# Two weighted products instead of three in every projection of a one-core block kernel

## The chip, the cores and the metric

The kernel runs on one core of one Trainium2 chip. The metric is the device time of one execution in microseconds. A second number, the span, is the time from the first to the last instruction of the profiled execution.

## The reference, cut to what matters

One layer of a hybrid block on 512 tokens of width 1024, all in fp32. A combined projection of the normed input feeds three branches; each branch has a projection of its own and a gate; their sum goes through an output projection. Then a layer of 16384 single-neuron experts follows, of which each token picks 128.

```python
proj = xn @ w_in[l]
(sb_q, sb_k, sb_v, ml_q, ml_k, ml_v, ml_i, ml_f, ml_o, mem_q, gate_pre) = jnp.split(proj, splits, axis=-1)
...
qk = jax.nn.silu(_causal_conv(jnp.concatenate([ml_q, ml_k], axis=-1), conv_w[l], conv_b[l]))
...
merged = (gates[:, :, 0] * (y_sb @ w_sb_o[l]) + gates[:, :, 1] * (y_ml @ w_ml_o[l])
          + gates[:, :, 2] * (y_mem @ w_mem_o[l]))
h = h + merged @ w_out[l]
hn = _rmsnorm(h, g_ffn[l])
h = h + _peer(hn, w_peer_q[l], peer_k1[l], peer_k2[l], peer_u[l], peer_v[l])
```

## The kernel before, in words

TensorE multiplies in fp32r, which keeps fewer bits than fp32. So each operand is cut in two: a high part (the value rounded to fp32r) and a low part (what is left). A projection adds three products for each block: high by high, high by low, low by high (the list `PARTS`).

The weights come in 101 items of 128 x 1024 values (512 KB). Item n passes through these hands:

- SyncE issues its load into one of four buffers `w_raw` (`load_item`, L507), once the low part of item n-4 is made.
- ScalarE makes the high part (`high_w`, L1263) in one of two buffers `w_r`, once item n-2 is multiplied: that item had the same buffer.
- GpSimd makes the low part (`low_ws`, L453), once the high part is there; for seven of the items VectorE does it (`DVE_LOW`, L1593).
- TensorE multiplies it with 24 products of 128 x 128 by 128 x 512 (12 where it works for the 256 memory tokens, 16 for item 20), and its end counts up `item_done`.

The stages follow one another on TensorE in a fixed order written into the program:

- Items 0 to 3 (L722, L731): keys of the memory tokens. Between them the input x is turned by TensorE, its high part made by ScalarE (L1286), its low part by VectorE (L1620). The row of 1/rms of the tokens then makes a round trip through DRAM (L528, L530) to stand on all partitions, in `rstd_b`; no projection is taken out of PSUM before it is there. SyncE loads item 8 and what follows behind that round trip.
- Items 4 to 19 (`t_item`, L741, L790): transposed projections, one PSUM bank each, four banks in turn. VectorE takes each out (L1633, L1660). Item 20 (L823) holds the input and forget gate columns.
- Items 21 to 36 (`n_item`, L754): natural projections. Meanwhile VectorE does the causal convolution of eight 128 x 512 groups (`conv`, L1646 and L1649, four instructions each), and ScalarE the silu.
- Items 37 to 44: memory values (L754) and gate items (L741) in turn. Gate items 4 to 23 are spread among the attentions as filler for TensorE: three for each of four pairs of stick-breaking heads, five in the mLSTM, three in the attention on memory.
- A head pair of the stick-breaking attention runs: scores on TensorE (L883, L887); Abs, Exp, Ln on ScalarE (L1337 to L1343); VectorE's `keep` (L1736); high part on ScalarE (L1347) and low part on VectorE (L1751); suffix sums on TensorE (L899); Exp on ScalarE (L1352).
- Items 65 to 76 (`branch`, L1027): the three branch projections. VectorE multiplies with the gates (L1878), adds up (L1885) and makes the low part (L1890).
- Items 77 to 84 (L754, L1048): output projection, then the second norm (L1905, L1454, L1914).
- Items 85 to 100 (L702, L741): query projection; key scores (L1102); top 16 lists on VectorE (L1955 to L1965).
- 128 `up` tiles of 16 products (L1141), of which `N_TOP` = 56 run while VectorE finishes its lists; GpSimd makes their low parts (L495). Then one-hot products (L1179) among 48 more `up` tiles, the rest of the `up` tiles, and 128 `down` tiles (L1150). These two already use two products with weighted parts.

A waiting instruction holds up all that stands behind it on its engine.

Of the kernel before, what the change touches and what calls it, by code (L numbers as in the profile page):

```python
# [60 lines left out]
N_TOP, PER_BLOCK = 56, 12  # L61
# [12 lines left out]
PARTS = ((0, 0), (0, 1), (1, 0))  # L74
# [22 lines left out]
def weights_of(n):  # L97
# [3 lines left out]
    if n <= I_IF:  # L101
        return n - I_T
# [9 lines left out]
SILU_AFTER = {3: (0, 1), 6: (2,), 7: (3,), 10: (4,), 11: (5,), 14: (6,), 15: (7,)}  # L112
EXP_AFTER, TURN_AFTER = (10, 20, 31, 44), (20, 33, 45, 52)
# [12 lines left out]
def build(nc, A, out, gates_dram, pre_dram, acts_dram):  # L126
    ctx = ExitStack()
    with ctx:
# [85 lines left out]
        x_two = carve_r("x_two", 34816, 4096)  # L214
        h_scaled = carve("h_scaled", 22528, 4096)
        junk = carve("junk", 43008, 1024)
        u_raw = [carve(f"uraw{s}", at, 1024) for s, at in enumerate((12288, 13312, 22528, 23552))]
        u_pairs = [carve_r(f"u_r{s}", at, 2048) for s, at in enumerate((24576, 10240, 18432, 20480))]
        act_stage = carve("act_stage", 8192, 2048)
        qryT = carve("qryT", 26624, 2048)  # L220
        keysT = carve("keysT", 28672, 2048)
        scores = carve("scores", 30720, 1024)
# [86 lines left out]
        x2 = x_two.rearrange("p (k t) -> p k t", t=T)  # L309
# [35 lines left out]
        if_low, f_sum = sem("if_low"), sem("f_sum")  # L345
# [47 lines left out]
        x2_made = sem("x2_made")  # L393
# [27 lines left out]
        def _(pool):  # L421
# [77 lines left out]
        def _(sp):  # L499
# [31 lines left out]
            with sp.Fori(2, I_IF // 4) as i:  # L531
                for s in range(4):
                    load_item(i * 4 + s, s, -I_T)
# [1045 lines left out]
        def _(dve):  # L1579
# [31 lines left out]
            for k in range(2, KD):  # L1611
                mem_low(k)
# [585 lines left out]
```

## Time and profile before

| what | value |
|---|---|
| time, median of 3 runs | 1636.06 us (1635.29 to 1636.38) |
| time outside the span (median less span) | 1.56 us |
| profiled execution: span | 1634.5 us |
| TensorE busy | 1627.7 us (100%), 8198 products |
| VectorE busy | 1088.1 us (67%) |
| ScalarE busy | 751.5 us (46%) |
| GpSimd busy | 406.9 us (25%), none after the first half |
| mean DMA rate | 211 GB/s |

The profiled execution is not timed by itself; its span is set beside the median. Busy is the time in which an engine works on at least one instruction. Products are pipelined, so the time from one to the next is read from long rows of them, and not from the mean of one.

### The profile page before, as it was taken

The numbers are of one execution on the slowest core, as the hardware profiler recorded it, in microseconds if no ns is written. First come the engines' busy times: TensorE is split into PE (matmuls) and PEld (weight loads), VectorE is DVE, ScalarE is ACT, GpSimd is POOL, SyncE is SP. The second block draws the span as 40 slices with busy tenths as digits, with TensorE's granted clock in tenths as the row PEclk, the third lists the DMA queues.
The fourth block names the chain that finished last, engine by engine and source line by source line (L and its number), as shares of the span: only waits on it lengthen the run. The fifth ranks groups of instructions, "written<-read, shape, count | busy, mean of one in ns | idle before, by whom it ended". The sixth has DMA issues, their size and how long they took to land.

```text
span 1634.5 us, 23689 instructions
## 1 busy us (share of the span) xinstructions
PE 1627.7 (100%) x8198; PEld 1348.8 (83%) x8198; DVE 1088.1 (67%) x1890; ACT 751.5 (46%) x939; POOL 406.9 (25%) x185
## 2 busy tenths in 40 slices
PE   9999999999999999999999999999999999999999
PEld 7888878788788888888888888888888888888887
DVE  4128443357483678999989999934466666666665
ACT  5223246644543434455445555555444444444442
POOL 5435433243253435777740000000000000000000
PEclk9999999999999999999999999999999999999999
DMA  6222242222542231666658888898698888888884
GB/s 235 95 103 92 102 156 96 97 78 97 201 170 100 103 130 61 223 213 213 216 213 292 320 298 308 295 321 296 236 321 293 280 286 292 297 285 286 291 288 156
DMA packets 166420, 344.68 MB, mean 211 GB/s; under 512 B 13260, under 2 KB 78796, under 8 KB 164048
## 3 DMA queue, kind: packets, MB, share of 16 engines
q1 hardware_dynamic: 166352, 343.79, 60.6%
q8 instruction: 41, 0.67, 0.2%
q14 instruction: 27, 0.22, 0.0%
HBM read 268.24 MB, written 75.51 MB: 210 GB/s over the span
## 4 chain that ended last, share of the span: by engine, by line
PE 98%; POOL 1%; ACT 1%; DVE 0%; issue 0%; ACTq 0%; POOLq 0%
PE ps L1150 28%; PE ps L1141 27%; PE ps L741 18%; PE ps L754 8%; PE ps L1027 4%; PE ps L1179 4%; PE ps L899 1%; PE ps L689 1%; PE ps L1102 1%; POOL u_r L495 1%; PE ps L1048 1%; PE ps L883 1%; PE ps L909 1%; PE ps L945 1%; PE ps L935 1%; PE ps L722 0%
## 5 line engine op out<-in xcount | busy, mean ns | idle before, releaser
L1150 PE MATMUL ps<-v_r,w_pairs 128*128 128x512 f32 x2036 | 461.7, 389 | 0.0
L1150 PEld LDWEIGHTS ps<-v_r,w_pairs 128*128 128x128 f32 x2036 | 382.3, 188 | 79.2
L1141 PE MATMUL ps<-hT_r,u_r 128*128 128x512 f32 x1024 | 400.7, 391 | 0.1
L1141 PE MATMUL ps<-x_two,u_r 128*128 128x512 f32 x1024 | 398.7, 389 | 0.0
L453 POOL TENSOR_TENSOR w_r<-w_raw,w_r 128x1024 fp32r<-128x1024 f32 x92 | 234.2, 2547 | 372.4 <-ACT w_r L1263 370.1
L2104 DVE TENSOR_TENSOR v_r<-vraw,v_r 128x1024 fp32r<-128x1024 f32 x128 | 156.9, 1226 | 150.2 <-ACT v_r L1560 150.2
L1560 ACT ACTIVATE v_r<-vraw 128x1024 fp32r<-128x1024 f32 x128 | 135.7, 1060 | 254.0 <-PE ps L1150 248.6
L1141 PEld LDWEIGHTS ps<-hT_r,u_r 128*128 128x128 f32 x1024 | 192.3, 188 | 40.4 <-POOL u_r L495 0.5
L1141 PEld LDWEIGHTS ps<-x_two,u_r 128*128 128x128 f32 x1024 | 192.3, 188 | 39.4
L741 PE MATMUL ps<-xT_r,w_r 128*128 128x512 f32 x936 | 218.6, 392 | 0.0
L1263 ACT ACTIVATE w_r<-w_raw 128x1024 fp32r<-128x1024 f32 x99 | 104.3, 1057 | 245.5 <-PE ps L741 132.0
L741 PEld LDWEIGHTS ps<-xT_r,w_r 128*128 128x128 f32 x936 | 174.1, 188 | 37.1 <-issue 1.2
L1507 ACT ACTIVATE act_stage<-ps 128x512 f32<-128x512 f32 x128 | 76.6, 598 | 226.3 <-PE ps L1141 226.3
L495 POOL TENSOR_TENSOR u_r<-uraw,u_r 128x1024 fp32r<-128x1024 f32 x56 | 160.0, 2865 | 47.9 <-ACT u_r L1488 47.8
L1488 ACT ACTIVATE u_r<-uraw 128x1024 fp32r<-128x1024 f32 x128 | 134.9, 1054 | 13.4 <-DMA uraw<-in_u 13.4
L2066 DVE TENSOR_TENSOR u_r<-uraw,u_r 128x1024 fp32r<-128x1024 f32 x72 | 87.5, 1223 | 63.3 <-ACT u_r L1488 63.2
L2100 DVE TENSOR_TENSOR w_f<-act_in,g_in 128x512 f32<-128x512 f32 x128 | 87.5, 684 | 7.0 <-issue 5.9
L2107 DVE SCALAR_TENSOR_TENSOR w_pairs<-w_pairs,w_f 128x512 fp32r<-128x512 f32 x128 | 87.5, 684 | 0.0
L754 PE MATMUL ps<-w_r,xT_r 128*128 128x512 f32 x384 | 87.2, 389 | 0.0
L754 PEld LDWEIGHTS ps<-w_r,xT_r 128*128 128x128 f32 x384 | 72.1, 188 | 14.9
L741 PE MATMUL ps<-hT_r,w_r 128*128 128x512 f32 x360 | 83.9, 391 | 0.0
L1562 ACT ACTIVATE w_pairs<-w_f 128x512 fp32r<-128x512 f32 x128 | 78.7, 615 | 3.4 <-DVE w_f L2100 3.4
(266 smaller groups left out, 1700.4 us busy)
## 6 DMA issues: line engine op xcount, KB each, us to landing
uraw<-in_u SPq DMA_DIRECT2D x128, 512.0 KB, 4.8
vraw<-in_v SPq DMA_DIRECT2D x128, 512.0 KB, 5.4
w_raw<-in_w SPq DMA_DIRECT2D x100, 512.0 KB, 3.7
acts_out<-act_stage SPq DMA_DIRECT2D x128, 256.0 KB, 2.3
gates<-stage SPq DMA_DIRECT2D x16, 2048.0 KB, 7.4
g_in<-gates SPq DMA_DIRECT2D x64, 512.0 KB, 6.4
act_in<-acts_out SPq DMA_DIRECT2D x128, 256.0 KB, 5.3
gates_pre<-pre_stage SPq DMA_DIRECT2D x24, 256.0 KB, 2.3
```

The costliest lines, as they stand in the source:

```text
L453: pool.tensor_tensor(wr4[:, n % 2, 1, :], raw3[:, n % 4, :], wr4[:, n % 2, 0, :].bitcast(F32), ALU.subtract).then_inc(w_lo_ready, 1)
L495: pool.tensor_tensor(u2[n % 4][:, 1, :], u_raw[n % 4], u2[n % 4][:, 0, :].bitcast(F32), ALU.subtract).then_inc(u_lo, 1)
L741: ins = pe.matmul(bank(b), wr4[:, s, ww, k * P:(k + 1) * P], act[:, wa, k, :], start=k == 0 and ww + wa == 0, stop=k == KD - 1 and ww == 1)
L754: ins = pe.matmul(bank(b0 + t), act[:, wa, 2 * j + k, t * P:(t + 1) * P], wr4[:, s, ww, k * BANK:(k + 1) * BANK], start=j == 0 and k == 0 ...
L1141: ins = pe.matmul(bank(s % 2), u2[s][:, w, k * P:(k + 1) * P], x2[:, k, :] if w else hr4[:, 0, k, :], start=i == 0, stop=i == 15, skip_gro ...
L1150: ins = pe.matmul(bank(2 * q + h), w2[:, s, w, q * P:(q + 1) * P], v2[s][:, w, h * BANK:(h + 1) * BANK], start=start and w == 0, stop=stop ...
L1263: act.activation(wr4[:, q % 2, 0, :], raw3[:, q, :], ACT.Copy).then_inc(w_hi_ready, 1)
L1488: act.activation(u2[s][:, 0, :], u_raw[s], ACT.Copy, scale=KEEP).then_inc(u_hi, 1)
L1560: act.activation(v2[s][:, 0, :], vr[:, s, :], ACT.Copy, scale=KEEP).then_inc(v_hi, 1)
L2066: dve.tensor_tensor(u2[s][:, 1, :], u_raw[s], u2[s][:, 0, :].bitcast(F32), ALU.subtract).then_inc(u_lo_dve, 1)
L2100: dve.tensor_tensor(wf[:, s % 2, :].rearrange("p (b t) -> p b t", t=BLK), ai3[:, s, :].rearrange("p (b t) -> p b t", t=BLK), g4[:, par, :, ...
L2104: dve.tensor_tensor(v2[s][:, 1, :], vr[:, s, :], v2[s][:, 0, :].bitcast(F32), ALU.subtract).then_inc(v_lo, 1)
```

## The change

- Every projection adds two products: weights times 1 - 1/128 rounded (high) by the high part of the activation, and the rest of the weights (low) by a second activation part that is weighted with 128 so that the two products add up to the full one. `PARTS` goes. High and low product of a block stand side by side on TensorE.
- For x and the memory tokens VectorE now makes the second part in two instructions (`x_low`, `x_two`; `mem_low`, `mem_two`), both with their own counters. Elsewhere it is one instruction, with other constants; the separate `x_two` of the expert layer goes.
- A new counter `hi_used` rises with the last high product of an item, `item_done` with the last low one. `high_w` waits for `hi_used` of item n-2 and for that item's low part; `low_ws` and `low_w` wait for `item_done` of item n-2.
- The transposed items come in another order: q and k of the mLSTM first. The convolution moves from among the natural items to among the transposed ones (`CONV_AFTER`), silu with it.
- Item 20 is an ordinary `t_item`.
- Weights of the second norm are applied on VectorE with a row `g_row`, loaded by two more DMAs.
- `N_TOP` is 60 for 56, the key scores have 8 slots for 2, the lists are turned later (`TURN_AFTER`), and query items use banks in another order.

```diff
-N_TOP, PER_BLOCK = 56, 12
+N_TOP, PER_BLOCK = 60, 12
...
-PARTS = ((0, 0), (0, 1), (1, 0))
...
-SILU_AFTER = {3: (0, 1), 6: (2,), 7: (3,), 10: (4,), 11: (5,), 14: (6,), 15: (7,)}
-EXP_AFTER, TURN_AFTER = (10, 20, 31, 44), (20, 33, 45, 52)
+CONV_AFTER = {3: 0, 4: 1, 6: 2, 7: 3, 9: 4, 10: 5, 12: 6, 13: 7}
+EXP_AFTER, TURN_AFTER = (12, 24, 36, 49), (22, 35, 47, 56)
+SCORE_SLOTS = 8
...
                         pool.wait_ge(w_hi_ready, o * 4 + n)
+                        pool.wait_ge(item_done, o * 4 + (n - 1))
                         pool.tensor_tensor(wr4[:, n % 2, 1, :], raw3[:, n % 4, :], wr4[:, n % 2, 0, :].bitcast(F32),
...
             sp.dma_start(rstd_p, acts_dram[1, 0, :].partition_broadcast(P)).then_inc(row_in, 16)
...
+            sp.dma_start(acts_dram[2, 0:2, :].rearrange("a b -> (a b)").rearrange("(p k) -> p k", k=KD),
+                         cols[:, C_FFN:C_FFN + KD]).then_inc(row_out, 16)
+            for n in range(8, I_IF + 8):
                 load_item(n, n % 4)
...
+            def t_part(s, b, act, w, made=None):
+
+                for k in range(KD):
+                    if made is not None:
+                        pe.wait_ge(made, k + 1)
+                    ins = pe.matmul(bank(b), wr4[:, s, w, k * P:(k + 1) * P], act[:, w, k, :],
+                                    start=k + w == 0, stop=k == KD - 1 and w == 1)
+                ins.then_inc((hi_used, item_done)[w], 1)
+
             def t_item(n, s, b, act, made_by_dve=1):
 
+                high_ready(n)
                 take_item(n, made_by_dve)
                 for k in range(KD):
-                    for ww, wa in PARTS:
-                        ins = pe.matmul(bank(b), wr4[:, s, ww, k * P:(k + 1) * P], act[:, wa, k, :],
-                                        start=k == 0 and ww + wa == 0, stop=k == KD - 1 and ww == 1)
-                ins.then_inc(item_done, 1)
...
+                    for w in range(2):
+                        ins = pe.matmul(bank(b), wr4[:, s, w, k * P:(k + 1) * P], act[:, w, k, :],
+                                        start=k + w == 0, stop=k == KD - 1 and w == 1)
+                        if k == KD - 1:
+                            ins.then_inc((hi_used, item_done)[w], 1)
...
-                    pe.wait_ge(memT_out, KD)
+                    pe.wait_ge(low_made, KD)
...
-                at_least(act, item_done, n - 1)
-                act.activation(wr4[:, q % 2, 0, :], raw3[:, q, :], ACT.Copy).then_inc(w_hi_ready, 1)
+                at_least(act, hi_used, n - 1)
+                if n >= 2:
+                    wait_low_w(act, n - 2)
+                act.activation(wr4[:, q % 2, 0, :], raw3[:, q, :], ACT.Copy, scale=KEEP).then_inc(w_hi_ready, 1)
...
+                high_w(n, n % 4)
+                g = CONV_AFTER.get(n - I_T - 4)
+                if g is not None:
+                    act.wait_ge(conv_done, g + 1)
+                    act.activation(projT3[:, 8 + g, :], conv_out[:, g % 2, :], ACT.Silu).then_inc(silu_done, 1)
...
+            def x_two(k):
+                dve.wait_ge(low_made, KD + k + 1)
+                dve.scalar_tensor_tensor(out=xr4[:, 1, k, :], in0=xr4[:, 1, k, :].bitcast(F32), scalar=SPREAD,
+                                         in1=xr4[:, 0, k, :].bitcast(F32), op0=ALU.mult, op1=ALU.add).then_inc(xT_out, 1)
+
+            x_low(0)
+            for k in range(1, KD):
+                x_low(k)
+                x_two(k - 1)
+            x_two(KD - 1)
...
+            for j in range(NT):
+                g = (j + 8) % NT
+                dve.wait_ge(item_done, I_T + j + 1)
...
+                if j in CONV_AFTER:
+                    conv(CONV_AFTER[j])
...
-                    dve.tensor_scalar(hs3[:, t, half], h3[:, t, half], rstd[:, c_], None, ALU.mult).then_inc(h_normed, 1)
+                    dve.scalar_tensor_tensor(out=hs3[:, t, half].rearrange("q (k p) -> q k p", p=P),
```

## Rows read from the trace of the kernel before

**Rows 1.** The page: TensorE's granted clock in 40 slices, in tenths (9 is 90% or more).

```profile
PEclk9999999999999999999999999999999999999999
```

**Rows 2.** The chain that ended last, in order of time: start, length, what.

```profile
29.58 81.60 PE ps L741 x360
...
845.13 3.69 PE ps L1179 x64
...
1167.15 461.49 PE ps L1150 x2036
```

**Rows 3.** Timeline, 55 to 75 us: start, length, engine, line, what, idle before.

```profile
56.88 1.06 ACT L1263 ACTIVATE w_r<-w_raw 128x1024 fp32r<-128x1024 f32 x1 [4.44 <-PE ps L741]
...
58.02 2.40 POOL L453 TENSOR_TENSOR w_r<-w_raw,w_r 128x1024 fp32r<-128x1024 f32 x1 [3.10 <-ACT w_r L1263]
...
56.95 0.69 DVE L1660 TENSOR_TENSOR projT<-ps,rstd_b 128x512 f32 x1 [4.76 <-PE ps L741]
```

**Rows 4.** Timeline, 100 to 202 us: VectorE's convolution beside GpSimd.

```profile
137.99 4.34 DVE L1649 SCALAR_TENSOR_TENSOR work<-projT,cols,work 128x509 f32<-128x509 f32 x3
...
146.73 2.32 DVE L1649 SCALAR_TENSOR_TENSOR work<-projT,cols,work 128x509 f32<-128x509 f32 x3
148.97 2.63 DVE L1646 TENSOR_SCALAR work<-projT,cols 128x512 f32<-128x512 f32 x1
...
137.80 2.40 POOL L453 TENSOR_TENSOR w_r<-w_raw,w_r 128x1024 fp32r<-128x1024 f32 x1 [2.44 <-ACT w_r L1263]
...
148.68 2.63 POOL L453 TENSOR_TENSOR w_r<-w_raw,w_r 128x1024 fp32r<-128x1024 f32 x1 [2.27 <-ACT w_r L1263]
```

**Rows 5.** Timeline of the start, 0 to 60 us.

```profile
19.91 1.85 ACT L1286 ACTIVATE xT_r<-ps,cols 128x512 fp32r<-128x512 f32 x3 [0.58 <-PE ps L689]
...
27.94 0.18 DVE L1624 RECIPROCAL rstd<-roots 128x4 f32<-128x4 f32 x1 [0.53 <-ACT roots L1291]
...
34.81 0.62 DVE L1630 COPY rstd_b<-rstd_p 128x512 f32<-128x512 f32 x1 [5.37 <-DMA rstd_p<-acts_out]
...
30.28 25.12 SPq L507 DMA_DIRECT2D w_raw<-in_w  x7
```

**Rows 6.** Timeline, VectorE at 543 us: its form with two SBUF inputs, nothing on GpSimd.

```profile
542.94 4.89 DVE L1944 SCALAR_TENSOR_TENSOR x_two<-hT_r 128x512 fp32r<-128x512 f32 x8
```

**Rows 7.** Timeline of one head pair, 289 to 315 us.

```profile
289.06 2.37 ACT L1337 ACTIVATE work<-ps 128x1280 f32<-128x1280 f32 x2 [1.50 <-PE ps L887]
...
302.74 1.48 DVE L1751 TENSOR_TENSOR lk_lo<-work,lk_hi 128x1280 fp32r<-128x1280 f32 x1
...
303.15 5.67 POOL L453 TENSOR_TENSOR w_r<-w_raw,w_r 128x1024 fp32r<-128x1024 f32 x2 [13.15 <-ACT w_r L1263]
...
306.62 5.70 PE L741 MATMUL ps<-xT_r,w_r 128*128 128x512 f32 x24
```

**Rows 8.** Timeline of the memory attention and the branches, 381 to 500 us.

```profile
403.04 1.23 DVE L1847 TENSOR_TENSOR work<-work,den 128x1024 f32<-128x1024 f32 x1
...
431.98 3.56 POOL L453 TENSOR_TENSOR w_r<-w_raw,w_r 128x1024 fp32r<-128x1024 f32 x1 [9.66 <-ACT w_r L1263]
...
453.49 3.48 DVE L1885 TENSOR_TENSOR mergedT<-mergedT,gate_s 128x512 f32<-128x512 f32 x2
...
424.20 16.04 PE L1027 MATMUL ps<-y_r,w_r 128*128 128x512 f32 x67
```

**Rows 9.** Timeline of output projection and second norm, 500 to 552 us.

```profile
524.21 1.23 DVE L1593 TENSOR_TENSOR w_r<-w_raw,w_r 128x1024 fp32r<-128x1024 f32 x1 [2.44 <-ACT w_r L1263]
...
536.03 0.88 DVE L1914 TENSOR_SCALAR h_scaled<-h_res,rstd 128x512 f32<-128x512 f32 x2
```

**Rows 10.** Lists: first and last instruction on VectorE; then its waits (us, times, longest).

```profile
551.54 0.88 DVE L1955 MAX8 top_lists<-scores 128x8 f32<-128x128 f32 x4 [3.71 <-ACT scores L1482]
...
825.37 2.15 DVE L2020 TENSOR_TENSOR top_small<-top_small 128x128 f32<-128x128 f32 x1
...
DVE top_lists L1955 <- ACT scores L1482: 22.6, 7, 6.7
```

More of the change, by code:

```diff
@@ L692, in take_item, with high_ready @@
                 wait_low_w(pe, n, made_by_dve)
-            def first_item(n, act, high, low, halves, begin):
-                def product(k, w, a):
-                    if not a and (k, w) in halves:
-                        pe.wait_ge(*halves[k, w])
-                    if not w:
-                        pe.wait_ge(low if a else high, k + 1)
-                    return pe.matmul(bank(0), wr4[:, n % 2, w, k * P:(k + 1) * P], act[:, a, k, :],
-                                     start=k + w + a == 0, stop=k + a == KD)
-                begin(product)
-                for k in range(2, KD):
-                    product(k, 0, 0)
-                    product(k, 1, 0)
-                    if k > 2:
-                        product(k - 1, 0, 1)
-                product(KD - 1, 0, 1).then_inc(item_done, 1)
+            def high_ready(n):
+                pe.wait_ge(w_hi_ready, n)
             def key_item(j):
@@ L748, in n_item @@
+            def n_item(n, s, j, b0, act, tiles, made=(None, None)):
+                high_ready(n)
                 take_item(n)
+                for w in range(2):
+                    if made[w] is not None:
+                        pe.wait_ge(made[w], j + 1)
                 for k in range(2):
-                    if landed is not None:
-                        pe.wait_ge(landed, (2 * j + k) // per + 1)
                     for t in range(tiles):
-                        for ww, wa in PARTS:
-                            ins = pe.matmul(bank(b0 + t), act[:, wa, 2 * j + k, t * P:(t + 1) * P],
-                                            wr4[:, s, ww, k * BANK:(k + 1) * BANK],
-                                            start=j == 0 and k == 0 and ww + wa == 0,
-                                            stop=j == 3 and k == 1 and ww == 1, skip_group_check=True)
@@ L758, in n_item @@
-                ins.then_inc(item_done, 1)
+                        for w in range(2):
+                            ins = pe.matmul(bank(b0 + t), act[:, w, 2 * j + k, t * P:(t + 1) * P],
+                                            wr4[:, s, w, k * BANK:(k + 1) * BANK],
+                                            start=j + k + w == 0, stop=j == 3 and k + w == 2, skip_group_check=True)
+                            if k == 1 and t == tiles - 1:
+                                ins.then_inc((hi_used, item_done)[w], 1)
@@ L818, in _ @@
             pe.wait_ge(proj_out, NT - 3)
-            take_item(I_IF)
-            pe.wait_ge(if_low, 1)
-            for k in range(KD):
-                for wa in range(2):
-                    ins = pe.matmul(bank(0), wr4[:, I_IF % 2, 0, k * P:(k + 1) * P], xr4[:, wa, k, :],
-                                    start=k == 0 and wa == 0, stop=k == KD - 1 and wa == 1)
-            ins.then_inc(item_done, 1)
+            t_item(I_IF, I_IF % 2, 0, xr4)
             for b in range(4):
@@ L1610, in _ @@
                               ALU.subtract).then_inc(w_lo_dve, 1)
+            mem_two(0)
             for k in range(2, KD):
                 mem_low(k)
+                mem_two(k - 1)
+            mem_two(KD - 1)
             dve.wait_ge(rooted, 1)
@@ L1617, in _, with x_low @@
                                      op1=ALU.mult, accum_out=sums[:, 2:3]).then_inc(squared, 1)
-            for k in range(KD):
+            def x_low(k):
                 dve.wait_ge(xT_hi, k + 1)
```

295 lines of the change are left out of this document (142 added, 153 removed).

## The prediction

> **What bounds the kernel now.** I read the page first: the reader is to see in the table TensorE busy for all of the span and no other engine above 67%, and the granted clock at its upper level in every slice [rows 1]. Then the chain that ended last, which shows that TensorE really is the path: long unbroken stretches of products, and 81.60 us for 360 of them in the projections, 461.49 us for 2036 in the down tiles. That is 0.2267 us from one product to the next in both [rows 2]. So each product that goes is worth 0.2267 us, as long as what feeds the next one is in time. An item of 24 products takes 5.44 us, one of 16 takes 3.63 us. The third view is the timeline, stage by stage, for how late each feeder may be; this is where the sum is decided, since the whole kernel stands at no slack at all and every stage loses a third of its cover.
>
> **What goes.** Keys 16 products, items 4 to 19 and 21 to 36 128 each, item 20 none, memory values 16, gates 192, branches 96, output 64, query 128: together 768. 768 x 0.2267 = 174.1 us. The expert layer's products stay as they are.
>
> **Feeding one item.** From the start of ScalarE's high part (1.06 us) to the end of GpSimd's low part (2.40 us) are 3.54 us [rows 3]. Both wait for item n-2, as they did, and TensorE now spends 3.63 us on item n-1 meanwhile. With 0.2 us for two semaphores, less 0.23 us since `hi_used` rises one product before the end, the chain is 3.5 us: just hidden. Anything that delays GpSimd by more than 0.1 us shows.
>
> **What delays GpSimd.** VectorE instructions with two SBUF inputs and GpSimd's low part exclude each other. One convolution step that began at 148.97, 0.29 us after GpSimd, took 2.63 us; three steps took 2.32 us alone and 4.34 us when GpSimd had begun first; and GpSimd itself took 2.63 instead of 2.40 us behind such a step [rows 4]. An eviction from PSUM isn't touched: 0.69 us [rows 3]. The Trainium skill (SBUF — State Buffer, Who interferes with whom) says the same in general: a VectorE instruction with two SBUF inputs and a GpSimd one that reads SBUF share a port as a lock, whoever is first. No row shows the new `x_two` and `mem_two` instructions, and by that page they are of the kind that waits.
>
> **Losses, stage by stage** (of what the 768 products give):
>
> *Start to item 7 (48 products, 10.9 us).* VectorE gets 16 more instructions. The nearest row is the old `x_two`, 8 in 4.89 us, 0.61 each, GpSimd idle [rows 6]; the bounds are 0.61 us and that plus the 2.1 us that a blocked step loses in rows 4. The memory ones are half as large, 8 x 0.35 = 2.8 us, and GpSimd is at work then; the turning of x waits for the last `mem_low`, so x comes some 2.8 us later than at 19.91 [rows 5]. From there VectorE has 8 x 0.69 + 8 x 0.65 = 10.7 us and, as I take it, two blocked steps (3.3 us together) and 0.7 us until the first high part: its reciprocal is at 19.9 + 2.8 + 14.7 = 37.4 instead of 27.94. Behind that reciprocal stands the round trip of 6.9 us [27.94 to 34.81, rows 5], and, worse, the load of item 8, issued 2.3 us after it at 30.28 [rows 5]. Now 37.4 + 2.3 + 0.4 for one more DMA issue = 40.1; it lands behind the broadcast, which alone took 5.2 us, so 5.8 us: 45.9; parts 3.6: item 8 begins at 49.5. Before it began at 29.42 + 3 x 5.44 = 45.7. All 10.9 us and 3.7 more are lost: 14.6. The bounds: no `x_two` blocked and the memory parts hidden gives 10; all blocked 18.
>
> *Items 8 to 20 (96 products, 21.8 us).* Eight convolutions now share 11 items with GpSimd's low parts. One after the other: 8 x (0.29 + 3 x 0.6, times after a block in rows 4) = 16.7, GpSimd 11 x 2.25 = 24.8, evictions not under a low part 11 x 0.6 = 6.6: 48.1 us. TensorE wants 11 x 3.63 = 39.9. ScalarE's silu stands before later high parts, and the low part of item 21 stands behind all this on VectorE. Loss 7 (bounds: 2 if order and slack absorb it, 16 if each step costs a whole block).
>
> *Items 21 to 36 (128, 29.0).* No convolution is left; loss 0.5.
>
> *Values and gates 0 to 3 (48, 10.9).* A gate item's low part is VectorE's, 1.23 us [rows 9]: chain 0.1 + 1.06 + 0.1 + 1.23 + 0.1 = 2.6 us, against a value item of 8 x 0.2267 = 1.8: 0.8 us four times, 3.2.
>
> *Stick-breaking (96, 21.8).* In a head pair ScalarE's chain starts with the scores (289.06) and ends in VectorE's last low part at 304.22. GpSimd, blocked by it from 303.15, ends two low parts at 308.82, the first by 304.2 + 2.3 = 306.5; TensorE began the third gate item at 306.62 [rows 7]. Nothing of that chain is shortened, so two shorter gate items before it are waited away and only the third pays: 1.8 us a pair, 2.3 in the first pair, where GpSimd is sooner. Gain 7.7, loss 14.1.
>
> *mLSTM (gates 16 to 19; 32, 7.3).* VectorE's steps between two products are two of 1.5 us, under a gate item of 3.63; loss 0.
>
> *Memory attention (32, 7.3).* VectorE works almost without a break until the shares are ready at 404.27 [rows 8], and TensorE turned them at once. Gates 20 to 22 pay 1.1 us of 5.4, gate 23 pays all. Loss 4.4.
>
> *Branches (96, 21.8).* The low part of the third item ended at 431.98 + 3.56 = 435.54, behind ScalarE's and VectorE's splits of the branch outputs [rows 8]. TensorE, which began at 424.20 [rows 8], now wants it 2 x 3.63 later, at 431.5: 4.1 us. From the second branch on two additions per item exclude GpSimd (3.48 us for two of 0.69 each [rows 8]); 2.25 + 1.3 us of port time plus gaps is 3.8 against 3.63, 8 times 0.2, and four 1.2 us low parts at the end, of which I take half: 7.7 in all.
>
> *Output (64, 14.5).* The low part of item 84 ends at 525.44 [rows 9], 8.0 us after item 81's end: ScalarE does four squares and a table load between. Wanted now 1.5 items after it, 5.4 us; 2.6 lost, 2.5 with `hi_used`.
>
> *Norm and first two query items (16, 3.6).* Norm steps go from 0.44 us [rows 9] to 0.61 or more [rows 6], 1.1 us for the two last tiles. ScalarE's eight high parts set the first item's end. Loss 2.6.
>
> *Other query items (112, 25.4).* Scores stand between them, so chains are hidden. VectorE's lists run unshared. Loss 0. The lists took 827.5 - 551.5 = 276 us, 22.6 of it waits for scores [rows 10]; with eight slots 253 + 7. TensorE has 845.1 - 551 = 294 us before its first one-hot product [rows 2], now 25.4 fewer and 4 x 3.63 = 14.5 more for `N_TOP`: 283. So 16 us remain for turning and one-hots, about 7 us. If that cover were gone, it would cost one for one. Moving four `up` tiles changes no product count. The `g_row` DMA lies 100 us ahead of its use.
>
> **Sum.** Losses 14.6 + 7 + 0.5 + 3.2 + 14.1 + 0 + 4.4 + 7.7 + 2.5 + 2.6 = 56.6. 174.1 - 56.6 = 117.5 off the span, 1634.5 to 1517.0; with 1.56 us outside, 1518.6. I say 1518.
>
> **Rivals.**
> - *Feeders keep up.* For: TensorE waits for nothing now, and several chains may start earlier as a whole. Against: rows 5 and 7 are chains without a product of a projection in them. Losses of half at most, 0 to 28 us: 1462 to 1490, 1475 as its middle. Chance 0.14.
> - *The clock falls.* My sum has eight waits of 2 to 4 us on TensorE, where now there is hardly one, and the clock stayed at 2.4 GHz [rows 1]. If after each the granted clock is 1.2 GHz for as long as one item, 3.6 us each, 29 us: 1547. The Trainium skill (TensorE: Matmul & The Clock Gate, Part 1) has an idle array fall to half rate and rise again after work; no row here shows a fall. Or the port costs whole blocks (16 and 18 in place of 7 and 14.6, and as much in the branches): 1535 to 1550. Together beyond 1535: 0.20.
> - *Slower than before.* Two `w_r` buffers make the feed a chain: if an item's parts took over 2 x 5.44 - 3.63 = 7.25 us, the projections would be slower than with three products. That needs GpSimd blocked for 3.7 us at every item; it happens to one in a few. At 8 us: (8 + 3.63)/2 - 5.44 = 0.4 us x 92 items, 1670. Chance 0.01.
>
> **How the numbers follow.** The forecast, 1500 to 1535 by its own bounds, has 0.65. For 8 in 10 the range takes most of the rivals beside it: 1487 to 1544. Within 0.2% or slower is out of reach of all but the last case (0.2% is about what a measurement of this kernel tells from no change): faster 0.98, same 0.01, slower 0.01.
>
> **What would show it.** Right: 7430 products; TensorE about 96% busy; 3.63 us items in 21 to 36; item 8 at 47 to 51 us with TensorE waiting for ScalarE or GpSimd; GpSimd's low part above 2.4 us among the convolutions; a gate item after suffix sums waiting for GpSimd; no wait at the first one-hot; from there to the end the old 789 us. Wrong: the first item of the natural projections before 94 us or after 110, head pairs below 22 us, or the granted clock below 1 in a slice.

## The result and the profile after

The changed kernel takes 1538.63 us in the median of 4 runs (1530.63 to 1539.46), the kernel before 1635.69 us beside it: a ratio of 0.9395, 95% interval 0.9374 to 0.9416 (the ratio comes from the single runs; that of the two medians would be 0.9407). Run again on another occasion (5 runs) it gave 1535.56 us, 0.9388 (0.9369 to 0.9407). So it is faster by 6%, and 20.6 us slower than the 1518 us I forecast. The profiled execution has a span of 1536.8 us, 97.7 less than before, where the 768 products alone are worth 174.1.

The page of the changed kernel, the lines that answer to [rows 1] and to the table of before:

```profile
PE 1486.2 (97%) x7430; PEld 1215.2 (79%) x7430; DVE 1100.2 (72%) x1890; ACT 749.8 (49%) x939; POOL 419.5 (27%) x188
...
PEclk8999999999989999999999999999999999999999
```

TensorE has 7430 products, as it should, but it is no longer busy all the time, and the row of the granted clock has two slices below 9. That is the first thing to see: in [rows 1] every slice was a 9. (A 9 stands for 90% or more, so a slice of 38 us can hide a short fall.)

The timeline of TensorE in the changed kernel: start, length, line, what, and in brackets the wait before it and what ended it. The rows are the first products of each stage and those behind its longer waits.

```profile
17.85 2.82 PE L690 MATMUL ps<-ident,xs 128*128 128x128 f32 x12 [2.83 <-DVE memT_r L1592]
...
30.95 1.11 PE L690 MATMUL ps<-ident,xs 128*128 128x128 f32 x4 [2.40 <-DVE xT_r L1622]
...
50.36 18.90 PE L738 MATMUL ps<-xT_r,w_r 128*128 128x512 f32 x80 [0.90 <-DVE projT L1673]
...
105.12 16.63 PE L754 MATMUL ps<-w_r,xT_r 128*128 128x512 f32 x64 [2.39 <-DVE w_r L1587]
121.95 44.82 PE L754 MATMUL ps<-w_r,xT_r 128*128 128x512 f32 x192 [0.20 <-POOL w_r L459]
166.61 2.03 PE L754 MATMUL ps<-w_r,memT_r 128*128 128x512 f32 x8
...
192.09 2.43 PE L871 MATMUL ps<-projT 64*128 64x512 f32 x16
...
198.07 10.23 PE L738 MATMUL ps<-xT_r,w_r 128*128 128x512 f32 x32 [3.00 <-DVE pre_stage L1707]
...
231.67 0.50 PE L887 MATMUL ps<-lk_hi,tri_r 128*128 128x512 f32 x1 [1.10 <-ACT lk_hi L1340]
...
233.96 0.50 PE L887 MATMUL ps<-lk_lo,tri_r 128*128 128x512 f32 x1 [1.03 <-DVE lk_lo L1756]
...
238.29 3.92 PE L738 MATMUL ps<-xT_r,w_r 128*128 128x512 f32 x16 [0.98 <-POOL w_r L459]
...
297.37 3.18 PE L923 MATMUL ps<-projT 128*128 128x512 f32 x10
...
329.61 1.91 PE L690 MATMUL ps<-ident,mem_q 128*128 128x128 f32 x16
...
346.47 1.29 PE L690 MATMUL ps<-ident,work 128*128 128x128 f32 x8 [1.87 <-DVE work L1853]
...
367.19 9.91 PE L1020 MATMUL ps<-y_r,w_r 128*128 128x512 f32 x40
378.55 5.81 PE L1020 MATMUL ps<-y_r,w_r 128*128 128x512 f32 x24 [1.45 <-POOL w_r L459]
...
415.04 3.89 PE L754 MATMUL ps<-w_r,merged_r 128*128 128x512 f32 x16
...
426.38 17.84 PE L754 MATMUL ps<-w_r,merged_r 128*128 128x512 f32 x64 [3.00 <-issue]
...
448.31 7.38 PE L1041 MATMUL ps<-w_r,merged_r 128*128 128x512 f32 x24 [2.16 <-DVE w_r L1587]
455.53 1.14 PE L690 MATMUL ps<-ident,h_scaled 128*128 128x128 f32 x9
459.31 0.33 PE L690 MATMUL ps<-ident,h_scaled 128*128 128x128 f32 x1 [2.64 <-DVE h_res L1915]
...
474.46 1.05 PE L1086 MATMUL ps<-keysT,qryT 128*128 128x128 f32 x8
...
541.33 83.68 PE L1139 MATMUL ps<-hT_r,u_r 128*128 128x512 f32 x368
...
761.75 3.85 PE L1177 MATMUL ps<-onehots 128*128 128x128 bf16 x64
```

From such starts, taken in both traces, comes the account by stages. Loss is what the removed products of the stage are worth less what the stage became shorter.

| stage | ideal | before | after | loss | forecast |
|---|---|---|---|---|---|
| start to item 8 | 10.9 | 45.7 | 50.4 | 15.5 | 14.6 |
| items 8 to 20 | 21.8 | 68.9 | 54.8 | 7.6 | 7 |
| items 21 to 36 | 29.0 | 87.0 | 61.5 | 3.5 | 0.5 |
| values, gates 0 to 3 | 10.9 | 33.2 | 25.5 | 3.1 | 3.2 |
| stick-breaking | 21.8 | 112.0 | 105.3 | 15.1 | 14.1 |
| mLSTM | 7.3 | 39.5 | 32.2 | 0 | 0 |
| memory attention | 7.3 | 37.8 | 37.6 | 7.0 | 4.4 |
| branches | 21.8 | 66.0 | 47.9 | 3.6 | 7.7 |
| output | 14.5 | 43.7 | 40.5 | 11.3 | 2.5 |
| norm, first query items | 3.6 | 15.4 | 18.9 | 7.1 | 2.6 |
| other query items | 25.4 | 90.6 | 66.9 | 1.6 | 0 |

The rest to the first one-hot product, 220.4 us for four more `up` tiles, and from there to the end, 775.05 us for four fewer, is 0.9 us off the counts of products. The table's losses add up to 75.4 us, with this 0.9 to 76.3, where I had 56.6. What stands behind the 20 us? The waits of TensorE in the first 480 us are 46 us together, less than the 56.6. The granted clock is the other part. The same kernel in stretches (columns: busy time and instructions by engine, then the granted clock):

```profile
195.00:198.00 3.00, 0.07 (x2) 0.00 (x0) 3.00 (x2) 2.90 (x3) 1.33 (x1) 0.84 0.00 0
198.00:202.00 4.00, 3.93 (x9) 3.14 (x10) 0.02 (x1) 3.97 (x4) 0.00 (x0) 0.50 0.61 197
259.00:261.00 2.00, 2.00 (x9) 1.90 (x8) 1.93 (x2) 1.98 (x3) 1.67 (x1) 0.50 0.02 4
426.00:432.00 6.00, 5.62 (x13) 4.46 (x14) 0.00 (x0) 0.00 (x0) 2.61 (x2) 0.50 0.54 178
450.00:453.00 3.00, 3.00 (x9) 2.32 (x8) 2.17 (x5) 2.03 (x6) 0.00 (x0) 0.50 0.28 112
460.00:466.00 6.00, 4.90 (x19) 3.40 (x20) 5.42 (x8) 3.55 (x9) 0.58 (x1) 0.50 0.74 262
```

0.50 is the lower level, 1.2 GHz. From 198 to 202 us TensorE did 9 products where 4 us at 0.2267 hold 17. Nine such stretches lie in the first 480 us; each begins in a wait of TensorE of 1.0 to 3.0 us or up to 1.3 us behind it; the share of the clock that is missing, summed over time, is 23.9 us.

### The profile page after: what moved, and what is told of

It reads as the page before. It is cut to its first block, busy times and chain, and to the rows that moved or that the text cites. A ratio compares the mean times of both kernels' runs of the same rounds, so it can differ in the third digit from the quotient of the medians.

```text
span 1536.8 us, 22224 instructions
## 1 busy us (share of the span) xinstructions
PE 1486.2 (97%) x7430; PEld 1215.2 (79%) x7430; DVE 1100.2 (72%) x1890; ACT 749.8 (49%) x939; POOL 419.5 (27%) x188
## 4 chain that ended last, share of the span: by engine, by line
PE 75%; DVE 15%; issue 4%; POOL 3%; ACT 1%; DMA 1%; SPq 0%; POOLq 0%; ACTq 0%; DVEq 0%
PE ps L1148 30%; PE ps L1139 24%; PE ps L738 6%; PE ps L754 5%; PE ps L1177 4%; POOL w_r L459 2%; DVE top_lists L1971 1%; DVE top_lists L1964 1%; POOL u_r L495 1%; DVE top_in L1965 1%; DVE top_lists L1968 1%; PE ps L690 1%; DVE top_lists L1961 1%; PE ps L887 1%; DVE h_scaled L1924 1%
## 5 line engine op out<-in xcount | busy, mean ns | idle before, releaser
L1139 PE MATMUL ps<-hT_r,u_r 128*128 128x512 f32 x2048 | 470.6, 390 | 0.1
L1139 PEld LDWEIGHTS ps<-hT_r,u_r 128*128 128x128 f32 x2048 | 382.7, 188 | 79.9 <-POOL u_r L495 0.5
L495 POOL TENSOR_TENSOR u_r<-uraw,u_r 128x1024 fp32r<-128x1024 f32 x60 | 172.9, 2893 | 46.6 <-ACT u_r L1481 46.4
L1263 ACT ACTIVATE w_r<-w_raw 128x1024 fp32r<-128x1024 f32 x99 | 104.0, 1055 | 139.3 <-PE ps L754 56.7
L738 PE MATMUL ps<-xT_r,w_r 128*128 128x512 f32 x624 | 152.9, 400 | 11.5 <-POOL w_r L459 5.1
L738 PEld LDWEIGHTS ps<-xT_r,w_r 128*128 128x128 f32 x624 | 116.7, 191 | 41.5 <-issue 11.5
L1481 ACT ACTIVATE u_r<-uraw 128x1024 fp32r<-128x1024 f32 x128 | 134.9, 1054 | 14.6 <-DMA uraw<-in_u 14.6
L1523 ACT ACTIVATE stage<-ps 128x1024 f32<-128x1024 f32 x64 | 61.9, 1019 | 5.0 <-PE ps L1177 5.0
L754 PE MATMUL ps<-w_r,xT_r 128*128 128x512 f32 x256 | 61.4, 400 | 2.6 <-DVE w_r L1587 2.4
L1177 PEld LDWEIGHTS ps<-onehots 128*128 128x128 bf16 x1024 | 58.8, 97 | 4.2 <-issue 4.2
L1177 PE MATMUL ps<-onehots 128*128 128x128 bf16 x1024 | 61.6, 218 | 0.0
L754 PEld LDWEIGHTS ps<-w_r,xT_r 128*128 128x128 f32 x256 | 48.2, 192 | 15.9 <-issue 6.0
```

The lines of the kernel that those rows point to most:

```text
L495: pool.tensor_tensor(u2[n % 4][:, 1, :], u_raw[n % 4], u2[n % 4][:, 0, :].bitcast(F32), ALU.subtract).then_inc(u_lo, 1)
L738: ins = pe.matmul(bank(b), wr4[:, s, w, k * P:(k + 1) * P], act[:, w, k, :], start=k + w == 0, stop=k == KD - 1 and w == 1)
L754: ins = pe.matmul(bank(b0 + t), act[:, w, 2 * j + k, t * P:(t + 1) * P], wr4[:, s, w, k * BANK:(k + 1) * BANK], start=j + k + w == 0, stop ...
L1139: ins = pe.matmul(bank(s % 2), u2[s][:, w, k * P:(k + 1) * P], hr4[:, w, k, :], start=i == 0, stop=i == 15, skip_group_check=True)
L1177: ins = pe.matmul(ps[:, at:at + P], oh_tiles[3 * s][:, q // PAIR, :, q % PAIR], oh_tiles[3 * s + 1 + w][:, q // PAIR, :, q % PAIR], start= ...
L1263: act.activation(wr4[:, q % 2, 0, :], raw3[:, q, :], ACT.Copy, scale=KEEP).then_inc(w_hi_ready, 1)
```

## The experiments

All but one edit are made to the changed kernel; times are medians beside the kernel before (1635.4 to 1635.6 us).

| label | edit | us | mean clock of the runs |
|---|---|---|---|
| after_again | none | 1535.56 | 0.984 to 0.991 |
| e1_clock | idle products (their result is read by nobody) in eight waits | 1526.39 | 0.997 to 0.999 |
| e2_fill | 48 idle products in head pairs | 1536.42 | 0.986 to 0.992 |
| e3_notaps | no two-input steps of the convolution (leaves most of it out) | 1527.18 | 0.989 |
| e4_notwo | second parts' second step on 8 columns (leaves the weighting out) | 1529.54 | 0.986 to 0.992 |
| e5_row | norm weights in order | 1532.60 | 0.985 to 0.993 |
| e6_queues | three queues in another order | 1528.30 | 0.989 to 0.993 |
| e8_half | low parts of items 22 to 36 half as wide (leaves the other half out) | 1531.07 | 0.990 |
| e9_waits | kernel before, three waits added | 1642.16 | 0.999 to 1.000 |
| e10_noidle | e6, e5, and a low part behind the norm | 1525.11 | 0.990 to 0.996 |
| e7_all | e10 and idle products | 1519.44 | 0.997 to 1.000 |
| e11_silu | silu one item later on ScalarE | 1537.12 | 0.984 to 0.989 |

**e1_clock.** Before each of the eight waits, for example at item 79:

```diff
+                    if b == 0 and j == 2:
+                        pe.wait_ge(br_used, 24)
+                        idle(13, 4, gr4[:, 0, 0, 0:P], gr4[:, 0, 0, :])
```

> The changed kernel with 86 idle products (same form as a projection's, into a free bank, result unused) put where TensorE waits 1.9 to 3.0 us: at about 15, 28, 103, 195, 345, 423, 446 and 456 us. No feeder is touched. Theory 1 (the missing 20 us are the granted clock, which fell to 0.50 behind these waits): the clock stays at 1.00 at these places and the time falls from 1538.6 to about 1520 (1516 to 1526). Theory 2 (the feeders set the pace and the half clock is only waited away): waits and places as before, 1535 to 1541. A feeder that is held up by the idle products would give more than 1541.

1526.39 us (1525.91 to 1527.98), ratio 0.9332 (0.9316 to 0.9347). TensorE does 86 products more and the kernel is 9 to 12 us faster. The stretches behind 195 us, in this kernel:

```profile
195.00:198.00 3.00, 3.00 (x13) 2.15 (x13) 0.38 (x1) 2.98 (x3) 0.00 (x0) 1.00 0.60 171
198.00:202.00 4.00, 4.00 (x20) 3.30 (x19) 2.59 (x3) 3.32 (x4) 0.00 (x0) 1.00 0.39 145
```

The clock stays up, and where 9 products went the four microseconds are full (the row counts 20, with those that overlap its ends). So the half clock costs time. Theory 1 holds in kind, but these idle products bring 9 to 12 us and not 20, and the time is just above its range of 1516 to 1526. The missing clock fell from 23.9 to 5.1 us, the span by 10.6: by these two executions some 0.6 of each us of clock is time, the rest waited away at the next feeder, as I take it (the table under e7 has other shares by stage). Three low stretches of 3 to 4 us were left, at 38, 253 and 448 us.

**e9_waits.** The kernel before, with

```diff
+                    if n in (25, 29, 33):
...
+                        for _ in range((n - 17) // 4):
+                            link(act.activation(wr4[:, n % 2, 0, :], raw3[:, n % 4, :], ACT.Copy))
```

> The kernel before (three products, clock at full in every slice), with ScalarE's high part of items 25, 29 and 33 held back by 2, 3 and 4 additional writes of the same values. By the slack of 1.9 us an item, TensorE should wait about 0.7, 2.0 and 3.2 us, together 5.9. Theory 1 (a wait of 2 us and more brings the clock to half for some us of the work behind it): granted clock 0.50 behind the second and third, time 1636 + 5.9 + 2 x 1.5 to 3.3 = 1645 to 1649. Theory 2 (a wait costs its own length): 1641 to 1643, clock 1.00.

1642.16 us (1641.14 to 1642.58), ratio 1.0040 (1.0026 to 1.0055). TensorE's timeline:

```profile
136.47 22.04 PE L754 MATMUL ps<-w_r,xT_r 128*128 128x512 f32 x96 [0.52 <-POOL w_r L453]
160.10 22.04 PE L754 MATMUL ps<-w_r,xT_r 128*128 128x512 f32 x96 [1.59 <-DVE ml_v L1695]
184.81 15.43 PE L754 MATMUL ps<-w_r,xT_r 128*128 128x512 f32 x67 [2.66 <-POOL w_r L453]
```

Waits of 0.5, 1.6 and 2.7 us, 4.8 together; the span of this execution is 4.9 us longer, and its clock 1.000. The median is in the range of theory 2. Theory 1 in its plain form falls: a wait of 2.7 us between long rows of products may pass without any fall, as in this execution. It need not: three of the five runs show 0.999 and take 1.2 us more on average, where all runs of the kernel before show 1.000; the profiled execution is not one of the three, so where their clock fell is not shown. In the changed kernel a wait of 2.4 us (105.12) did bring the fall. What decides it is not settled by these runs.

**e2_fill.** Eight idle products ahead of each gate item before the suffix sums in pairs 1 to 3 (`gate_item(m, 8 if p else 0)`).

> The changed kernel with 8 idle products more (the third product's place) in each of the two gate items before the suffix sums of head pairs 1 to 3: 48 products, 10.9 us of TensorE. Theory (the pair's own chain from scores to low part sets its length; TensorE waits 1.1 + 1.0 + 1.0 us a pair): the waits go, 0.5 us a pair is left over, 1538 to 1541. Rival (TensorE's work sets the length of a pair): 1549.

1536.42 us, as fast as without them; the stage takes 105.5 us where it took 105.3, and the only wait of 0.2 us or more left in it is the 3.0 us before its first gate item. 10.9 us of TensorE's work cost nothing: the pair's own chain sets its length, as the prediction had it.

**e3_notaps.** `conv` ends behind its first instruction.

> The changed kernel without the three two-input additions of each convolution (24 instructions; only the first tap is computed, so this leaves out most of the convolution). Theory (they and GpSimd's low parts exclude each other, and the low part of item 21 stands behind them): TensorE's waits among items 8 to 21, 0.7 + 0.7 + 1.5 + 2.4 us, and the half clock behind the last are gone, 1538.6 - 5.3 - 2.2 = 1531, item 21 at about 98 us instead of 105.1. Rival (ScalarE's order or the loads hold the items): item 21 within 1 us of 105, 1538.

1527.18 us; item 21 begins at 97.82 us. VectorE is the third number in these rows, the changed kernel first, this one second:

```profile
50.36:105.12 54.76, 49.19 (x209) 38.41 (x209) 53.88 (x47) 19.50 (x24) 30.45 (x13) 1.00 0.37 125
```

```profile
50.00:97.80 47.80, 47.80 (x206) 37.65 (x205) 14.57 (x21) 18.41 (x22) 28.20 (x12) 1.00 0.43 144
```

VectorE was busy for 53.88 of 54.76 us, and without the 24 steps for 14.57. In the changed kernel's timeline these steps take 35.2 us, 1.5 each with the locks, where three that nothing holds up take 2.32 [rows 4]. VectorE was the bound of this stage: from item 8 (49.08) to item 21 are 48.7 us instead of 54.8. This is more than the 5.3 us of waits that the theory counted there, and the time fell by 8.4 to 11.5 us.

**e11_silu.** `CONV_AFTER.get(n - I_T - 4)` on ScalarE becomes `- 5`.

> The changed kernel with each silu of the convolution one weight item later in ScalarE's order, nothing else. Theory (ScalarE waits 3.8 to 4.5 us for a convolution to end while the data of the next high part is there, and the low part and TensorE wait behind it: the queue passes the lock on): the 3.0 us of waits for GpSimd among items 8 to 20 are mostly gone, from item 8 to item 21 52 to 53 us instead of 54.8, time 1533 to 1537 by what of the half clock goes with them. Rival (GpSimd and VectorE shut each other out for so long that the order on ScalarE doesn't matter): 54.3 to 55.3 us from item 8 to item 21, time unchanged.

1537.12 us. My theory fell; the stage came out 0.3 us above the rival's range too. The waits for GpSimd among these items went from 3.1 to 0.2 us, and item 21 came no sooner:

```profile
93.42 7.89 PE L738 MATMUL ps<-xT_r,w_r 128*128 128x512 f32 x32 [1.26 <-DVE projT L1670]
105.95 6.40 PE L754 MATMUL ps<-w_r,xT_r 128*128 128x512 f32 x15 [4.65 <-DVE w_r L1587]
```

From item 8 to item 21 are 55.6 us. The wait moved to the low part of item 21, which is VectorE's own. ScalarE's order only chose where the wait for VectorE shows.

**e4_notwo.** The second steps `x_two` and `mem_two` on columns 0 to 7.

> The changed kernel with the second instruction of the activations' second part on 8 columns instead of 256 or 512 (x_two, mem_two; this leaves the weighting of the second part out, the 16 instructions and all waits stay). Theory (these two-input instructions on VectorE, and GpSimd's lock on them, make the start late): the last one ends some 8 us earlier than 38.6, item 8 begins at 42 to 45 us instead of 50.4, time 1530 to 1533, less where the half clock behind the waits at 15 and 28 us goes too (1527). Rival (the weights' own parts or the round trip set the start): item 8 within 1 us of 50.4, 1538.

1529.54 us; the row of TensorE at item 8:

```profile
44.41 18.83 PE L738 MATMUL ps<-xT_r,w_r 128*128 128x512 f32 x80 [0.98 <-ACT w_r L1263]
```

6.0 us sooner than in the changed kernel, as the theory has it. Six other runs with the same start have item 8 between 48.16 and 50.37, so the gain is 3.8 to 6.0 us. The wait at 28 us fell from 2.4 to 0.2. That at 15 us stayed (2.55), and it is the lock's, which 8 columns don't remove. GpSimd had begun a low part, and `mem_two` on 8 columns stood behind it for 2.17 us, and with it the last `mem_low` that TensorE waits for:

```profile
13.24 2.37 POOL L459 TENSOR_TENSOR w_r<-w_raw,w_r 128x1024 fp32r<-128x1024 f32 x1
```

```profile
13.47 2.17 DVE L1598 SCALAR_TENSOR_TENSOR memT_r<-memT_r 128x8 fp32r<-128x8 f32 x1
```

**e8_half.** `low_ws(I_IF + 2, I_KV - 1 - I_IF, BANK)`, 512 of 1024 columns.

> The changed kernel with GpSimd's low parts of items 22 to 36 on half of their width (this leaves half of these low parts out). Theory (the feed of an item, high part 1.06 and low part 2.40 us with their handovers, takes 3.72 us and sets the pace there, not the products): 3.63 us an item instead of 3.72, 1.3 us less in all. Rival (0.1 us is lost on TensorE itself between two items): 3.72 as before.

```profile
104.85 58.29 PE L754 MATMUL ps<-w_r,xT_r 128*128 128x512 f32 x256 [2.35 <-DVE w_r L1587]
162.97 2.03 PE L754 MATMUL ps<-w_r,memT_r 128*128 128x512 f32 x8
```

58.12 us for 16 items, 3.63 each. In the changed kernel the last 12 took 44.66, 3.72 each: there the feed sets the pace. (The single time of this run is no evidence: half clocks differ from run to run.)

**e5_row.** The row is stored by blocks and read in order:

```diff
-                                             in1=g_row.rearrange("q (p k) -> q k p", k=KD)[:, 4 * b:4 * b + 4, :],
+                                             in1=g_row[:, half],
```

> The changed kernel with the row of the second norm's weights laid out block by block, so that VectorE reads it in order (it reads every eighth value now); its store to DRAM stands behind the load of item 23. Theory (the stride is what makes one norm step 1.16 us long where I took 0.61): 0.6 to 0.7 us each, the waits in the norm fall by 1 to 3 us, time 1534 to 1537. Rival (two inputs and a scalar by partition cost 1.16 us in any layout, or GpSimd's lock is the cost): 1.16 us, time unchanged.

1532.60 us (1528.61 to 1538.00), ratio 0.9373 (0.9348 to 0.9399): not to be told from the changed kernel by the time. By the trace it is; the changed kernel first (duration ns min/median/max):

```profile
L1924 DVE SCALAR_TENSOR_TENSOR h_scaled<-h_res,rstd,g_row x8: 1146/1164/3246, 451.8 to 464.0; 128x512 f32<-128x512 f32 x8
```

```profile
L1925 DVE SCALAR_TENSOR_TENSOR h_scaled<-h_res,rstd,g_row x8: 743/752/2854, 449.0 to 458.2; 128x512 f32<-128x512 f32 x8
```

The stride costs 0.41 us each (a step in order takes 0.75, not 0.6 to 0.7); the maximum, a step that GpSimd's low part of item 85 locks out, stays. The stage of the norm went from 18.9 to 16.9 us, but the clock has a share in that: in the changed kernel its mean over this stage was 0.82, in this execution 1.00. How much of the 2.0 us is the stride's is open.

**e6_queues.** Three moves: `take_gate(3)` ahead of the scaling of the memory keys on VectorE; the parts of item 84 ahead of the four squares on ScalarE and VectorE; and on ScalarE

```diff
+            high_w(I_OUT + 2, (I_OUT + 2) % 4)
             merged_hi(3)
```

> The changed kernel with three steps of a queue in another order, nothing else: VectorE takes gate 3 out before it scales the memory keys; ScalarE makes the high part of item 79 before it waits for the last merged block; the parts of item 84 are made before the four squares and the table load. Theory (three of TensorE's waits, 3.0 at 195, 3.0 at 423 and 2.2 at 446 us, are work queued ahead of what is wanted): 3.0 + 3.0 + 1.8 us of waits and 4.8 us of half clock behind the last two, 1538.6 - 12.6 = 1526 (1522 to 1531). Rival (the next chain takes each wait over: the suffix sum's parts, the low part of item 79, the norm's first root): 1535 to 1539.

1528.30 us (1525.15 to 1531.26), ratio 0.9350 (0.9334 to 0.9366). The output stage went from 40.5 to 32.7 us, but a wait of 2.8 us now stands before the first suffix sums, 1.5 before item 79 for VectorE's last merged block, and 3.57 in the norm:

```profile
444.32 1.33 PE L690 MATMUL ps<-ident,h_scaled 128*128 128x128 f32 x5 [3.57 <-DVE h_scaled L1925]
```

So theory and rival both hold in part. The wait at 446 us was the queue's (2.2, now 0.3); the one before item 79 was so by half (3.0, now 1.5); the first one only moved; and the stage of the norm became 2.1 us longer, 21.0.

**after_again, e10_noidle, e7_all.** e10 is e5 and e6 together, with GpSimd's `low_ws(I_PQ, 1)` behind `wait_ge(h_normed, 2 * TT)`. e7 is e10 with 57 idle products in six waits.

> The changed kernel as it is, to see how far its own executions lie apart. Both theories: 1530 to 1540. If the clock behind waits is what differs from one execution to the next, its time falls with the mean granted clock over the runs (0.984 to 0.991 so far), by about 1 us for each 0.001 x 1536 = 1.5 us of half clock undone or less, since part of it is waited away.

> The changed kernel with the three queues in the other order and the row of the second norm laid out block by block, and with GpSimd's low part of item 85 behind the norm steps that it locks out (the wait of 3.6 us at 441 us of the run with the three queues). Theory: 2 us from the row and 2 from the lock on top of that run's 1528.3: 1524 (1520 to 1528). Rival (item 85's later low part holds up the first query items): 1528 or more.

> The kernel of the run before this one (its label ends in noidle) with 57 idle products in the six waits of 1.5 to 2.9 us that it should have left, at about 15, 28, 103, 200, 340 and 415 us. Theory (the granted clock falls behind such waits, with a chance that differs by place and execution): 4 to 8 us less, 1518 (1514 to 1522), and executions closer together. Rival (what is left of the half clock is waited away): within 1 us of it.

1535.56 (1531.75 to 1541.33), 1525.11 (1520.14 to 1526.07) and 1519.44 us (1518.59 to 1520.50), on the same chip, 5 runs each; ratios 0.9388, 0.9323 (0.9310 to 0.9335) and 0.9291 (0.9278 to 0.9303). In after_again the time falls with the mean clock, 1541.33 at 0.984 and 1531.75 at 0.991, as expected; in e10 it doesn't (1520.14 at 0.994, 1525.11 at 0.996). e10 and e7 are in the ranges of their theories. In e10 no norm step is locked out any more:

```profile
L1926 DVE SCALAR_TENSOR_TENSOR h_scaled<-h_res,rstd,g_row x8: 744/748/752, 438.6 to 445.6; 128x512 f32<-128x512 f32 x8
```

e7 is the fastest kernel of the study, 16 us below the changed one, and its five runs lie within 2 us where those of the changed one lie 10 apart. Its profiled span is 1517.1 us; against the ideal it loses 174.1 - 117.4 = 56.7 us, what I forecast in all. That is chance and confirms nothing: it is another kernel, with other queues and filled waits.

These runs also price the clock without any idle product, since the same wait brought the fall in one execution and not in another. Stage lengths, none with an idle product in that wait:

| stage | wait | clock fell | clock stayed up |
|---|---|---|---|
| items 21 to 36 | 2.4 | 61.5 to 61.6 (changed, again, e2, e4) | 60.0 to 60.1 (e5, e6, e10) |
| memory attention | 1.9 | 37.5 to 37.6 (changed, again, e2, e5) | 35.9 (e3, e4, e6, e8, e10, e11) |
| stick-breaking, first gate item | 3.0 | 105.1 to 106.7 (changed, again, e2, e3, e4, e5, e11) | 103.3 (e8) |

The row of e8 with its wait of 3.0 us, and the clock behind it:

```profile
194.41 7.55 PE L738 MATMUL ps<-xT_r,w_r 128*128 128x512 f32 x32 [3.02 <-DVE pre_stage L1707]
```

```profile
195.00:199.00 4.00, 4.00 (x19) 3.32 (x18) 0.62 (x2) 3.97 (x4) 0.00 (x0) 1.00 0.60 197
```

So a fall costs some 1.4 to 2 us in these stages (the 106.7 is e4, whose clock fell in three later pairs too), and the length of the wait alone does not decide whether it comes.

## Why the prediction was right and where it was wrong

The 1538.63 us lie inside the range for 8 in 10 (1487 to 1544), but outside the 1500 to 1535 that I gave the forecast itself, and one of my signs of being wrong came true: the granted clock fell below 1 in a slice. So the range was right with the help of its rivals.

**Right: the account by stages for waits.** The start (14.6 against 15.5), items 8 to 20 (7 against 7.6), values and gates (3.2 against 3.1), stick-breaking (14.1 against 15.1), mLSTM (0) and the part behind the query items (0 against 0.9) came out within 1 us or so. The mechanisms were tested: VectorE's new steps make the start late (e4), the chain of a head pair sets its length (e2), VectorE with its lock sets items 8 to 20 (e3, e11). Item 8 began at 50.4, in the 47 to 51 us I named, and behind the load of item 8, for which ScalarE waited:

```profile
46.69 1.06 ACT L1263 ACTIVATE w_r<-w_raw 128x1024 fp32r<-128x1024 f32 x1 [8.08 <-DMA w_raw<-in_w]
47.83 2.38 POOL L459 TENSOR_TENSOR w_r<-w_raw,w_r 128x1024 fp32r<-128x1024 f32 x1 [3.70 <-ACT w_r L1263]
```

The low part ends at 50.21 and item 8 begins at 50.36 (the profile names VectorE as what ended this wait, but its eviction of the bank, the first of four that take 2.47 us from 48.38, was over by then). Yet the load was not the price that I made it: TensorE was at items 6 and 7 until 49.45, and only 0.9 us is the load's. Item 6 itself came late, behind VectorE's steps, and behind two half-clock stretches of 7 us each that the sum did not have. In e6, where the clock stayed up until 36 us, item 8 began at 48.16: there the start loses 13.3 us. So the 14.6 is near by some luck.

The 7 for items 8 to 20 is near by luck too. Its own sum gives 48.1 - 39.9 = 8.2, and it has the convolution's steps at 0.6 us where three take 2.32 [rows 4], and GpSimd's low parts at 2.25 where the rows show 2.40; neither 0.6 nor 2.25 can be read there. Also, the step read at 148.97 [rows 4] is the convolution's first instruction, which reads one tile in SBUF and not two. It was held up as well, as four of its eight are in the changed kernel (1.77 to 2.63 us, the others 0.54).

One sign was off by a slip: from the first one-hot product to the end I named the old 789 us, where 775.05 were measured. The four `up` tiles that moved ahead are 14.5 us, which the sum had added before that product and forgot behind it; the total is not touched.

**Wrong: "the clock stayed at 2.4 GHz".** The sum took 0.2267 us for every product behind a wait as well. I had the fall as a rival, at 3.6 us for each of eight waits, 29 us, with 0.20 together with the port. It happened at nine places and cost 9 to 12 us by e1 and 6 by e7 against e10, which has fewer waits to fill. The sum of the prediction itself made the waits; the same sum should have carried their second cost at a share. The page TensorE: Matmul & The Clock Gate of the Trainium skill (Part 1, HAM oscillation) has bursts of products between waits start at half rate each time, and says that products arranged without these gaps keep the full rate. The trace agrees in kind, 0.50 behind nine waits and 1.00 where they were filled; e9, with 2.7 us and no fall, and e8, with 3.0, show that a wait of this size need not bring it.

**Wrong: output, 2.5 against 11.3.** I looked at item 84 alone, and its wait came as forecast (2.16 at 448.31). ScalarE's high part of item 79 stood behind its wait for the last merged block:

```profile
421.76 1.06 ACT L1432 ACTIVATE merged_r<-mergedT 128x1024 fp32r<-128x1024 f32 x1 [4.68 <-DVE mergedT L1894]
422.73 1.99 ACT L1263 ACTIVATE w_r<-w_raw 128x1024 fp32r<-128x1024 f32 x2
```

ScalarE idles 4.68 us while the data of the high part lies there. That block was late in turn: one `merged_lo` before it took 3.42 us beside GpSimd's low part (1.21 alone). e1 and e6 divide the stage: 40.5 as it is (mean clock 0.87), 36.1 with idle products and the clock at 1.00, 32.7 with the other queue and the clock at 1.00.

**Wrong: norm, 2.6 against 7.1.** I had 0.61 us a step from [rows 6]; it is 1.16, and once 3.2 behind GpSimd. The stride is 0.41 of it (e5). The page SBUF — State Buffer of the Trainium skill (Door 1: The DMA port swizzle) says that SBUF is read in lines of 16 bytes, and that each access in a new line costs; every eighth fp32 value is in a new line, and 0.75 against 1.16 agrees. A half clock of 7 us came on top; what each cost of the 4.5 us is not divided by these runs.

**Wrong by little.** Items 21 to 36, 3.5 against 0.5. One feed in the changed kernel; the item before ended at 144.16:

```profile
144.16 3.52 PEld L754 LDWEIGHTS ps<-w_r,xT_r 128*128 128x128 f32 x16 [0.19 <-issue]
144.26 1.06 ACT L1263 ACTIVATE w_r<-w_raw 128x1024 fp32r<-128x1024 f32 x1 [2.67 <-PE ps L754]
...
145.40 2.40 POOL L459 TENSOR_TENSOR w_r<-w_raw,w_r 128x1024 fp32r<-128x1024 f32 x1 [1.35 <-ACT w_r L1263]
...
147.91 3.50 PEld L754 LDWEIGHTS ps<-w_r,xT_r 128*128 128x128 f32 x16 [0.23 <-issue]
```

From 144.16 to 147.91 are 3.75 us, not 3.5: 1.06 and 2.40, 0.29 for three handovers, and no sign of the 0.23 that I took off for `hi_used`. Over 16 items the feed costs 2.0 us (60.1 where the clock stayed up, 58.1 in e8), and the half clock at 105 us the other 1.4. Memory attention, 7.0 against 4.4: 35.9 us in place of 37.6 where the clock stays up, so 1.7 of the miss is the clock.

**Wrong the other way: branches, 7.7 against 3.6.** The low part of the third item ended 11.3 us into the stage, as in the kernel before (378.50 - 367.19, 435.54 - 424.20). But I had TensorE wait for it with the whole item. In the changed kernel a branch item does its 8 high products first and waits for the low part only then: 40 products stand before the wait at 378.55, not 32. That takes 8 x 0.2267 = 1.8 us off my 4.1. Behind it 1.3 us were lost where I had 3.6 for the port and the last low parts. This miss in the other direction kept the total from being off by 24.

The rivals: feeders that keep up (1475) are out, and so is slower than before. The changed kernel's medians, 1538.63 and 1535.56, lie in the region of the rival with the clock or the port, beyond 1535. Its clock half happened, at less than half of its 29 us; the port at whole blocks did not (7.6 where it had 16).

## What to carry to other kernels

Where a change takes work from an engine that never waits, it makes waits, and on TensorE these can have a second price in its clock: read the clock row after the change, and try products whose result nobody reads in the waits. Before pricing a feeder, walk the whole queue of each engine ahead of it: an instruction that waits for another stage's data holds up one that has its own. Where moving a wait moves it only to the next step, ask which engine has no idle time in that stretch.

## What the runs showed of the hardware that was not expected

- Half clock in stretches of 3 to 7 us in or behind waits of 1.0 to 3.0 us, at places that differ between executions: the runs of the changed kernel have mean clocks of 0.984 to 0.991 and times of 1530.6 to 1541.3 us, the two with 0.991 the shortest of each occasion. A wait of 2.7 us in one execution of the kernel before (e9) and one of 3.0 us in e8 brought none.
- A VectorE step on 8 columns waited as long for GpSimd's low part as a step on 256: 2.17 us (e4) and 2.19 us (changed kernel, 14.49).
- The convolution's first instruction, with one tile in SBUF as input, took 1.77 to 2.63 us beside GpSimd's low part and 0.54 otherwise.
- A step with two SBUF inputs on VectorE takes 0.75 us for 128x512 read in order and 1.16 us with one input read at every eighth value.
